# The norm behind attention computed by rows, in a two-layer streaming encoder on one core

## What is computed

```
q, k, v, u = split(h @ w_in)                      # attention heads and a pooling mixer
mix = concat(diff_attention(q, k, v), pool_mixer(u))
h = layer_norm(ALPHA * h + mix @ w_out, ln1_g, ln1_b)     # the norm behind attention
h = layer_norm(ALPHA * h + moe_ffn(h), ln2_g, ln2_b)      # 16 experts, top 2 inside one group
layer_norm: y = (x - mean) * rsqrt(var + 1e-5) * g + b    # over the 1024 columns of a row
```

## Time and profile before

| | |
|---|---|
| three runs | 1044.29, 1045.44, 1042.64 us; median 1044.29 |
| profiled execution | 1044.27 us |
| its span, first to last instruction | 1042.5 us |
| TensorE matmul busy | 969.9 us (93%), 5132 instructions |
| VectorE busy | 833.4 us (80%), 1206 instructions |
| ACT busy | 654.1 us (63%), 927 instructions |
| GpSimd busy | 253.7 us (24%), 337 instructions |
| mean granted TensorE clock | 0.955 of full |
| the norm behind attention runs | from 149 to 210 us (layer 0), from 670 to 718 us (layer 1) |

### The profile page before, as it was taken

One profiled execution on the slowest core, in us unless ns is written; L12 is line 12 of the kernel. 1 busy time (PEld: TensorE's weight loads), 2 busy tenths in 40 slices (PEclk: granted clock), 3 DMA queues, 4 the chain that ended last, 5 costly groups with the idle time before them and its releaser, 6 DMA issues.

```text
span 1042.5 us, 15247 instructions
## 1 busy us (share of the span) xinstructions
PE 969.9 (93%) x5132; PEld 800.2 (77%) x5132; DVE 833.4 (80%) x1206; ACT 654.1 (63%) x927; POOL 253.7 (24%) x337
## 2 busy tenths in 40 slices
PE   4999889999999999999939999898899999999993
PEld 4988767777888888888739987687688888888882
DVE  7867657859989989899773675677799989898995
ACT  5355431248888888888543454314688888888881
POOL 1223533443111111110211235425211111111022
PEclk8999899889999999999959998996999999999997
DMA  9558820588999999996971334318899999999964
GB/s 352 179 170 258 271 85 26 204 296 304 359 368 368 369 357 355 377 368 241 282 255 53 107 125 175 132 37 318 318 354 374 365 361 368 374 357 348 347 196 123
DMA packets 118318, 278.28 MB, mean 267 GB/s; under 512 B 8771, under 2 KB 11067, under 8 KB 118238
## 3 DMA queue, kind: packets, MB, share of 16 engines
q1 hardware_dynamic: 99648, 240.40, 64.5%
q0 software_dynamic: 11040, 21.14, 7.0%
q10 hardware_dynamic: 7566, 15.96, 4.4%
HBM read 266.51 MB, written 30.37 MB: 285 GB/s over the span
## 4 chain that ended last, share of the span: by engine, by line
PE 80%; DVE 13%; issue 3%; ACT 2%; POOL 1%; DMA 0%; ACTq 0%; DVEq 0%; POOLq 0%
PE PS L968 22%; PE PS L644 12%; PE PS L1007 11%; PE PS L973 11%; PE PS L1011 6%; PE PS L949 3%; PE PS L815 1%; PE PS L816 1%; PE PS L817 1%; PE PS L989 1%; DVE w_lo L1391 1%; DVE stats L1128 1%; PE PS L587 1%; DVE N L1140 1%; DVE w_lo L1182 1%
## 5 line engine op out<-in xcount | busy, mean ns | idle before, releaser
L1391 DVE TENSOR_TENSOR w_lo<-ring,w_hi 128x1024 fp32r<-128x1024 f32 x256 | 303.6, 1236 | 41.5 <-ACT w_hi L1886 39.0
L1886 ACT ACTIVATE w_hi<-ring 128x1024 fp32r<-128x1024 f32 x256 | 260.8, 1059 | 50.3 <-PE PS L1011 27.1
L968 PE MATMUL PS<-w_hi,x_hi 128*128 128x512 f32 x512 | 165.6, 405 | 3.0 <-ACT w_hi L1886 3.0
L973 PE MATMUL PS<-w_lo,x_hi 128*128 128x512 f32 x512 | 163.3, 400 | 3.1 <-DVE w_lo L1391 3.0
L968 PE MATMUL PS<-w_hi,x_lo 128*128 128x512 f32 x512 | 162.3, 398 | 0.4 <-DVE x_lo L1381 0.4
L1398 DVE TENSOR_TENSOR w_lo<-ring,w_hi 128x1024 fp32r<-128x1024 f32 x128 | 154.4, 1220 | 4.3 <-ACT w_hi L1899 4.3
L1899 ACT ACTIVATE w_hi<-ring 128x1024 fp32r<-128x1024 f32 x128 | 135.3, 1059 | 30.2 <-PE PS L973 28.5
L973 PEld LDWEIGHTS PS<-w_lo,x_hi 128*128 128x128 f32 x512 | 96.4, 190 | 28.6 <-DVE w_lo L1391 6.6
L968 PEld LDWEIGHTS PS<-w_hi,x_lo 128*128 128x128 f32 x512 | 97.5, 191 | 24.5 <-DVE x_lo L1381 1.7
L2191 POOL DMA_INDIRECT M<-xs,idx x30 | 51.4, 1715 | 255.5 <-PE PS L949 242.4
L968 PEld LDWEIGHTS PS<-w_hi,x_hi 128*128 128x128 f32 x512 | 95.0, 191 | 24.2 <-issue 1.8
(11 more groups left out here) (247 smaller groups left out, 1632.9 us busy)
## 6 DMA issues: line engine op xcount, KB each, us to landing
ring<-in_w_gate SPq DMA_DIRECT2D x32, 2048.0 KB, 14.7
ring<-in_w_up SPq DMA_DIRECT2D x32, 2048.0 KB, 15.3
ring<-in_w_down SPq DMA_DIRECT2D x32, 2048.0 KB, 14.8
ring<-in_w_in SPq DMA_DIRECT2D x8, 2048.0 KB, 17.8
ring<-in_w_out SPq DMA_DIRECT2D x4, 2048.0 KB, 8.3
ys<-H SPq DMA_DIRECT2D x2, 3072.0 KB, 20.0
H<-ys POOLq DMA_DIRECT2D x12, 512.0 KB, 8.2
M<-in_cache_k ACTq DMA_DIRECT2D x8, 512.0 KB, 3.8
```

The lines of the kernel that those rows point to most:

```text
L968: pe.matmul(PS[:, n, :], x[:, c:c + P], w_hi[j][:, k * 512:(k + 1) * 512], start=(j == 0 and k == 0 and x is x_hi[par]), stop=False)
L973: mm = pe.matmul(PS[:, n, :], x_hi[par][:, c:c + P], lo[:, k * 512:(k + 1) * 512], start=False, stop=(j == 3 and k == 1))
L1391: dve.tensor_tensor(lo, w, w_hi[j][:, :].bitcast(F32), ALU.subtract).then_inc(up_lo, 1)
L1886: act.activation(w_hi[j][:, :], quarter(3 * par + n, j)[0], ACT.Copy).then_inc(up_hi, 1)
```

## The change

In the norm behind attention (q = 1 and 3):

- The residual addition also gives the row sum; one short operation gives minus the mean and tells `mean_done`. `ln_front`, `ln_z`, `ln_h_gain` and `ln_h_shift` are no longer called there.
- ACT sums the squares (`squared_rows`), for tile 0 behind `xo_split(l, "decode")`, for others behind the exponential of the tile before. The squares themselves go to `M[:, 4416:5440]`, the memory of `V`.
- GpSimd's `row_power` (two operations, with a wait between them) takes the place of `ln_power`.
- VectorE's `gained` and `shifted` make the finished rows ahead of the transposes; TensorE transposes `H` itself, on `h_done`; VectorE and ACT copy four blocks with one plain copy each. `seat` of the tile before moves ahead of VectorE's copy.
- Gain and shift are loaded into `gb_two` from SP's queue, behind the loads of expert 1, with waits for attention's last scores and products; ACT's two loads go.
- GpSimd's memset of `M[:, 0:2048]` moves from behind the first power to behind the last `rows_out`, and its wait for `cv_used` goes.

```diff
-        square_rows = M[:, 2048:3072]
+        square_rows = {1: M[:, 4416:5440], 2: M[:, 2048:3072], 3: M[:, 4416:5440], 4: M[:, 2048:3072]}
-        Z1 = [N[:, 2816 + 1024 * i:3840 + 1024 * i] for i in range(2)]
...
+        def mean_count(q, n):
+
+            return ln_count(q, n) - len(order(0))
...
                     load_up(l, 1, 3, E0 + 1, [d[3], (proj_ps, 16 * (l + 1))])
+                    sp.wait_ge(score_ps, BASE[l] + 12)
+                    sp.wait_ge(av_ps, 12 * (l + 1))
+                    for k, row in ((0, t["ln1_g"][l]), (1, t["ln1_b"][l])):
+                        sp.dma_start(gb_two[:, k, :], row.partition_broadcast(P)).then_inc(gb_in, 16)
                     load_up(l, 0, 0, E0, [projected] * 2)
...
-                pe.wait_ge(z_done, turned + 1)
+                if q in LN1:
+                    pe.wait_ge(h_done, ln_count(q, n))
+                else:
+                    pe.wait_ge(z_done, turned + 1)
...
-                z = z_of(q)[n % 2]
+                z = H[:, j, :] if q in LN1 else Z2[n % 2]
...
+                if q in LN1:
+                    bank = turned_at(q, n, 0)[0]
+                    dve.tensor_copy(FT[:, 0:4, TC[j]:TC[j] + TN[j]],
+                                    PS[:, bank, :].rearrange("p (k n) -> p k n", k=4)[:, :, 0:TN[j]]).then_inc(hx_dve, 1)
+                    return
...
-                    c = did(dve.scalar_tensor_tensor(H[0:rows, j, :], H[0:rows, j, :], ALPHA,
-                                                     PS[0:rows, b:b + 2, :].rearrange("p k n -> p (k n)"), ALU.mult,
-                                                     ALU.add))
+                    h = H[0:rows, j, :].rearrange("p (b n) -> p b n", b=2)
+                    c = did(dve.scalar_tensor_tensor(h, h, ALPHA, PS[0:rows, b:b + 2, :], ALU.mult, ALU.add,
+                                                     accum_out=stats[0:rows, j, 12:13]))
                     after(c)
                     dve.sem_inc(res_done, 1)
-                    ln_front(q, j)
+                    dve.tensor_scalar(stats[0:rows, j, 13:14], stats[0:rows, j, 12:13], -1.0 / D, None, ALU.mult
+                                      ).then_inc(mean_done, 1)
                     if n == 0 and l == 0:
                         o_scale(l, 12)
-                    ln_z(q, n)
-                    if n >= 1:
-                        ln_h_gain(q, n)
-                    turned_h(q, n)
-                    if n == 0:
-                        ln_h_gain(q, n)
-                    ln_h_shift(q, n)
+                    shifted(q, n, gained(q, n))
                     if n >= 1:
                         seat(l, n - 1)
+                    turned_h(q, n)
                     choose(l, n)
...
+                if q in LN1:
+                    bank = turned_at(q, n, DVE_TURNS)[0]
+                    act.activation(FT[:, 4:8, TC[j]:TC[j] + TN[j]],
+                                   PS[:, bank, :].rearrange("p (k n) -> p k n", k=4)[:, :, 0:TN[j]], ACT.Copy
+                                   ).then_inc(hx_act, 1)
+                    return
...
-                load_gb(LN1[l], t["ln1_g"][l], t["ln1_b"][l])
                 mixed(l, 11)
                 xo_split(l, "decode", ("o", 11))
                 last = len(order(LN1[l])) - 1
                 for n, j in enumerate(order(LN1[l])):
+                    squared_rows(LN1[l], n)
                     if n == last:
                         k_rows(l, (0, 1))
                     turned_h(LN1[l], n)
...
-                    ln_power(LN1[l], n)
-                    if n == 0:
-                        if l == 0:
-                            xo_rest(l, "meta")
-                        pool.wait_ge(cv_used, HEADS * (l + 1))
-                        pool.memset(M[:, 0:2048], 0.0).then_inc(xg_zero, 1)
+                    row_power(LN1[l], n)
+                    if n == 0 and l == 0:
+                        xo_rest(l, "meta")
                     if n >= 1:
                         share(l, n - 1)
                         rows_out(l, n - 1)
                 rows_out(l, len(tiles) - 1)
+                pool.memset(M[:, 0:2048], 0.0).then_inc(xg_zero, 1)
                 share(l, len(tiles) - 1)
```

More of the change, by code:

```diff
@@ L398, in xo_count @@
             return len(XO) * l + list(XO).index(what) + 1
-        def z_of(q):
-            return Z1 if q in LN1 else Z2
         def order(q):
@@ L1139, in ln_z @@
                     dve.wait_ge(hx_ps, 2 * (TURNED[q] + n) - 2)
-                dve.tensor_scalar(z_of(q)[n % 2][0:rows], H[0:rows, j, :], st[:, 12:13], st[:, 15:16], ALU.subtract,
+                dve.tensor_scalar(Z2[n % 2][0:rows], H[0:rows, j, :], st[:, 12:13], st[:, 15:16], ALU.subtract,
                                   ALU.mult).then_inc(z_done, 1)
@@ L1515, in mean_taken, with gained, shifted @@
                 dve.tensor_scalar(st[:, 13:14], st[:, 12:13], -1.0 / D, None, ALU.mult).then_inc(mean_done, 1)
-            def gained(l, n):
-                j = order(LN2[l])[n]
+            def gained(q, n):
+                j = order(q)[n]
                 p = slice(0, TN[j])
                 if n == 0:
-                    dve.wait_ge(gb_in, 32 * (LN2[l] + 1))
-                dve.wait_ge(mean_done, sum_count(l, n))
+                    dve.wait_ge(gb_in, 32 * (q + 1))
+                dve.wait_ge(mean_done, mean_count(q, n))
                 return did(dve.scalar_tensor_tensor(gained_rows[n % 2][p], H[p, j, :], stats[p, j, 13:14],
                                                     gb_two[p, 0, :], ALU.add, ALU.mult))
-            def shifted(l, n, c):
-                j = order(LN2[l])[n]
+            def shifted(q, n, c):
+                j = order(q)[n]
                 p = slice(0, TN[j])
                 after(c)
-                dve.wait_ge(ln_rstd, ln_count(LN2[l], n))
+                dve.wait_ge(ln_rstd, ln_count(q, n))
                 dve.scalar_tensor_tensor(H[p, j, :], gained_rows[n % 2][p], stats[p, j, 15:16], gb_two[p, 1, :],
@@ L1656, in _ @@
                     if n >= 1:
-                        shifted(l, n - 1, gain_at[n - 1])
+                        shifted(LN2[l], n - 1, gain_at[n - 1])
                     if n >= 2 and l + 1 < DEPTH:
                         turned_rest(l, n - 2)
-                    gain_at.append(gained(l, n))
+                    gain_at.append(gained(LN2[l], n))
                 if l + 1 < DEPTH:
                     w_split(l + 1, 0)
-                shifted(l, last, gain_at[last])
+                shifted(LN2[l], last, gain_at[last])
                 if l + 1 < DEPTH:
@@ L1673, in _ @@
         def _(act):
-            def load_gb(q, g, b):
-                for k, row in ((0, g), (1, b)):
-                    act.dma_start(gb[:, k, :], row.partition_broadcast(P)).then_inc(gb_in, 16)
             def load_ck(l, h):
@@ L1716, in w_split, with squared_rows @@
                 act.activation(wp(n), list(w_chunk(m))[0], ACT.Copy).then_inc(wp_hi_done, 1)
-            def squared_rows(l, n):
-                j = order(LN2[l])[n]
+            def squared_rows(q, n):
+                j = order(q)[n]
                 p = slice(0, TN[j])
-                act.wait_ge(mean_done, sum_count(l, n))
+                act.wait_ge(mean_done, mean_count(q, n))
                 if n >= 1:
-                    act.wait_ge(ln_var, ln_count(LN2[l], n - 1))
-                act.activation(square_rows[p], H[p, j, :], ACT.Square, bias=stats[p, j, 13:14], accum_out=stats[p, j, 14:15]).then_inc(ln_var, 1)
+                    act.wait_ge(ln_var, ln_count(q, n - 1))
+                act.activation(square_rows[q][p], H[p, j, :], ACT.Square, bias=stats[p, j, 13:14], accum_out=stats[p, j, 14:15]).then_inc(ln_var, 1)
             def turned_hi(l, n):
@@ L2075, in _ @@
                 for n in range(len(tiles_of(l))):
-                    squared_rows(l, n)
+                    squared_rows(LN2[l], n)
                     if l + 1 < DEPTH and n >= 2:
@@ L2112, in h_prepared, with row_power @@
                 last.then_inc(h_scaled, 1)
-            def row_power(l, n):
-                j = order(LN2[l])[n]
+            def row_power(q, n):
+                j = order(q)[n]
                 st = stats[0:TN[j], j, :]
-                pool.wait_ge(ln_var, ln_count(LN2[l], n))
+                pool.wait_ge(ln_var, ln_count(q, n))
                 then(pool.tensor_scalar(st[:, 14:15], st[:, 14:15], 1.0 / D, EPS, ALU.mult, ALU.add))
@@ L2310, in _ @@
                 for n in range(len(tiles_of(l))):
-                    row_power(l, n)
+                    row_power(LN2[l], n)
 _INS = ["x_prompt", "x_sample", "cache_k", "cache_v", "state_pool", "meta_tokens", "ln_in_g", "ln_in_b", "w_in",
```

## The result

The changed kernel took 1050.65 us in the median of six runs (1048.86 to 1052.12), the kernel before 1043.94 us beside it; the ratio is 1.0059 with a 95% interval of 1.0033 to 1.0085. A later sample of twelve runs gave 1050.53 us and 1.0056 (1.0031 to 1.0082). So it is slower by about 6 us.

What follows compares the result with a forecast made beforehand. The prediction took the expert stretch as bound by TensorE and the output projection's ring as set by latency between addition and transposes. Its terms summed to 4.2 us: 1044.27 + 4.2 = 1048.5 us, range 1044.8 to 1052.0.

Steps and rivals of the forecast that it cites:

- The middle tile: Output projection with norm: addition to transposes 5.18 us against 4.64, +0.54 us for each of three tiles, 1.62 us.
- my third rival: Memset misses the choice and the 0.51 us gap behind layer 0's second addition goes: 1047.3 us; 23 in 100.
- The first tile: Transposes later: +1.70 us in layer 0, where squares stand behind ACT's decode mixing and split; +0.23 in layer 1.
- The last tile: GpSimd's moved memset runs into the choice and can hold VectorE: +0.35 us in layer 0, +0.3 in layer 1.
- the forecast mask of 13.1 us: Layer 0's last tile: the choice's mask, ready at 11.3 us without the memset, comes at 13.1 with it.
- The sum: Whole kernel: 1.70 + 1.08 + 0.35 in layer 0, 0.23 + 0.54 + 0.3 in layer 1, 4.2 us slower.
- the expert stretches unchanged in length: Expected sign in the profile after: the expert stretches, where TensorE is busy throughout, keep their length.
- The clock in the tail: Rival: TensorE's clock stays at 1.00 in the tails instead of 0.50, 6.7 us back, 1041.7 us; 10 in 100.
- the first rival: TensorE's clock falls oftener through longer waits; one fall over 12 projection matmuls adds 2.8 us, 1051.5; 15 in 100.
- The rival of two SBUF inputs at half speed: The shift takes twice its 1.28 us in each of 7 tiles, 9 us more: 1057.5 us; 1 in 100.

Runs made afterwards that it cites:

- pad29: Changed kernel with 29 one-element memsets more on VectorE at its very start, nothing else: 1048.25 us, ratio 1.0034.
- a_sq: Changed kernel with the first tile's squares and power ahead of the last attention unit's work, and its gain ahead of the output scale: 1046.68 us, ratio 1.0018.
- memset_late: Changed kernel with GpSimd's memset of the gather buffers behind the last tile's share instead of ahead of it: 1049.14 us, ratio 1.0034.
- b_pad48: Kernel before, without the change, with 48 one-element memsets at the start of VectorE: 1049.03 us, ratio 1.0025.
- a_pad16: Changed kernel with 16 one-element memsets at the very start of VectorE: 1046.92 us, ratio 1.0024.
- act_loop: a_sq plus 29 VectorE start memsets, with ScalarE's skipped code 73 instructions shorter and 55 semaphore increments on ScalarE ahead of layer 1's first squares: 1045.58 us, ratio 1.0022.
- all_four: Changed kernel with the edits of a_sq, pad29, act_loop and memset_late together: 1042.29 us, ratio 0.9976; once more, 1045.11 us, ratio 1.0003.

## Why the prediction was right, and where it was short

The direction and the range held: 1050.65 us against 1048.5, within 1044.8 to 1052.0. By its steps:

- **The middle tile**, +0.54 us each: 15.00 - 14.45 = 0.55 us in layer 0's third tile, and 15.02 against 14.46 in layer 1's. In all traces of the changed order it is 15.00 to 15.03, but for pad29's second tile (15.32). The step was right to a hundredth, as its parts came from rows of the same form. In layer 0's second tile the stray gap of 0.51 us that my third rival spoke of did go, so that it grew by only 0.18 us (14.83 to 15.01); that part of the rival was right.
- **The first tile**, +1.70 us in layer 0: 157.63 against a forecast of 157.6, and a_sq shows the cause by removing it. (The working, 153.96 + 3.60 - 155.91, gives 1.65, and 0.20 for layer 1; the sum took 1.70 and 0.23.) Layer 1, +0.23: 17.12 against 16.95 from addition to addition, 0.17.
- **The last tile**, +0.35 and +0.3 us: this term had the wrong sign in layer 0. The memset did fall into the choice and hold a VectorE operation, for 1.37 us more than its 0.22. But the forecast mask of 13.1 us behind the addition was too late on two counts: it charged the whole 1.81 us of the memset, and it had the choice ready at 11.3 without it, where memset_late's rank matmul ran at 11.05 without waiting. The rank matmul came at 12.24 us, 0.46 earlier than before (12.22 to 12.25 in six more traces with the memset in this place). That the first expert matmul came 18.74 us behind the addition, 1.3 later than before, is TensorE's clock: the next 16 matmuls of `first_x` took 3.75 us against 2.02. b_pad48, without the change, had 18.60. In layer 1 the memset held nothing: the operations of the choice that ran beside it were of other forms, and in the other traces with the memset in this place VectorE ran nothing beside it.
- **The sum** of 4.2 us: the steps that the traces can separate give 1.79 + 0.18 + 0.55 - 0.46 in layer 0 and 0.17 + 0.56 in layer 1, 2.8 us, against 3.9 forecast for them; layer 1's last tile is lost in the clock. So it is luck that the kernel after was 3.1 us late at the last split of layer 0, as forecast: 2.1 us are steps, the lower clock of `first_x` added 1.7, and the way through the experts was 0.6 shorter. Without the two stalls the medians are 1046.9 (a_pad16) and 1048.2 us (pad29), 3 to 4.8 us above the kernel before; with the uncertainty of 1.5 to 2 us they fit 4.2 and 2.8 alike.
- **What failed** is what has no term in the sum: it ends with the norm and takes it that behind it nothing moves ("the expert stretches unchanged in length"). The stretches did keep their length, but at their end the loss of 26 and 45 instructions moved VectorE's jump so that it starts one piece earlier but still ends in the same one, in both layers. This missing term is 2.3 to 3.7 us by the medians and 2.6 + 1.2 us by the distances of the profiled execution, a third or more of the result. Direction and range would have held without it too. No view of the profile before shows it: it is in how many instructions an engine's program has, and in the jump behind the experts, whose cost there, if any, was hidden under 1.63 and 1.06 us of other waits.
- **The rivals.** The clock in the tail did stay up once, in the profiled execution's layer 1 (17.16 us), which the prediction had named as a sign of being wrong; none of the eleven other traces of this order shows it (19.6 us or more), and the two of the order before had 20.46 and 22.12. That the clock fell at the start of layer 1's output projection in the same execution is the first rival's kind of event; one execution doesn't show that the change brings it. The rival of two SBUF inputs at half speed is out: the shift took 1.27 or 1.28 us in all tiles of the kernel after.

That the code's position sets the stall is shown by the edits. That it is a fetch of code, by the instruction queue, is argued: it rests on the queue's packets in the gap and on their 8 KB. The shift of 60 is fitted, not explained, and so is the size of 128 in part. The Trainium skill, "Runtime: NRT & Kernel Launch", section "Instruction fetch mechanics", says that an engine fetches ahead in sequence only, and that a taken branch out of the two pages at hand stalls for the fetch; by that rule the traces agree. It gives the pages 256 instructions (16 KiB); with these VectorE's 213 could never leave the current page and the next, so with both at hand no stall of VectorE could come, and the traces show it. Either the pieces are smaller here (128, as the packets and act_loop suggest), or the next page wasn't there yet; no run on VectorE tells the two apart.

## What to carry to other kernels

Where an engine's program has a taken branch (skipped rounds, a conditional block) in a place that the other engines wait on, count the instructions of that engine when it is changed anywhere ahead of it, and look at the idle time behind the branch before and after: an edit that only shortens the code can cost microseconds there, and a few dummy instructions in an idle place can give them back (16 or 29 here, but not 6 or 48). Read such a stall by its length; the releaser that the profile names may be data that arrived at the same time. And where single executions differ by 5 us through TensorE's clock, compare stages between landmarks of the traces, not medians alone.

## What the runs showed of the hardware

- A jump over 198 or 199 instructions on ScalarE cost 0.3 us in layer 0 and nothing that shows in layer 1; one over 261 or 264 cost 4.8 to 6.3 us wherever the profile names no wait for data.
- GpSimd's memset of 128x2048 (1.82 us) holds VectorE's tensor_scalar of 16x4 until it ends: 1.57 to 1.62 us instead of 0.22 in eight traces, 1.10 in a_sq. It doesn't hold small operations of other forms: in layer 1 of the kernel after, a scalar_tensor_tensor in its middle took its usual time. Nor does it hold a tensor_scalar of 128x32 that reads PSUM (0.17 us in all_four).

```profile
718.96 1.83 POOL L2299 MEMSET M<- 128x2048 f32 x1
...
719.73 0.24 DVE L1308 SCALAR_TENSOR_TENSOR N<-N,CT 128x16 f32<-128x16 f32 x1
...
720.09 0.16 DVE L1311 TENSOR_TENSOR N<-N 128x8 f32<-128x8 f32 x1
```

- It goes the other way too. A GpSimd operation on 16x2 elements, 0.18 us when alone in memset_late, took 3.90 us in the kernel after under VectorE's splits:

```profile
211.44 3.90 POOL L2214 TENSOR_TENSOR N<-N 16x2 f32<-16x2 f32 x1
...
211.81 3.48 DVE L1403 TENSOR_TENSOR w_lo<-ring,w_hi 128x1024 fp32r<-128x1024 f32 x3
```

- 55 semaphore increments on ScalarE took 4.2 us, 0.08 us each: padding is only free where the engine is idle for as long.
